# Nine more projections as seven block products, with a ring of three weight slots

## The reference

```
# first block
h = norm(x);  proj = h @ w_in            # q_a k_a v_a q_i k_i w_i z_a c_q c_kv k_rope z_b q_m z_m gates(3*1024)
o_a = top-k sparse attention(q_a, k_a, v_a; index from q_i, k_i, w_i)
o_b = causal attention(norm(c_q) @ w_uq, norm(c_kv) @ w_ukv, k_rope)
kv_m = norm(mem) @ w_mem_kv;  o_m = attention(norm(q_m), norm(k_m), v_m)
branch_n = (o_n * silu(z_n)) @ w_branch[n]
merged = sum_n sigmoid(gate_n) * branch_n
x = x + merged @ w_out
# second block
u = norm(x);  dq, dk, dv, gq, gk, gv, gg, gr = split(u @ w_in_2)
z = gr @ gate_w + gate_b;  log_a = log_sigmoid(z) / 16
L = cumsum(log_a in chunks of 64);  Lc = L - L[middle]
a = where(lower, (q e^Lc)(k e^-Lc)^T, (q e^-Lc)(k e^Lc)^T)
og = a @ v + inter-chunk state;  gla = norm(og) * silu(gg)
da = softmax attention(q1,k1,dv) - lam * softmax attention(q2,k2,dv), q and k normed by heads
x = x + concat(norm(da), gla) @ w_o
x = x + cross_attention(norm(x), norm(mem_2), w_cq, w_ckv) @ w_co
x = x + hierarchical_moe(norm(x))        # 32 experts, top 2 in the best of 4 groups, 1024 -> 512 -> 1024
```

## Time and profile before

| | |
|---|---|
| Median of the runs | 1144.57 us (1144.38 to 1144.93) |
| Profiled execution | 1144.48 us |
| Its span | 1142.8 us |
| PE busy | 944.0 us, 83% of the span, 4742 records |
| DVE busy | 341.3 us, 30% |
| ACT busy | 175.3 us, 15% |
| POOL busy | 102.6 us, 9% |
| DMA | 290.33 MB, 254 GB/s over the span |

### The profile page before, as it was taken

How to read it: one execution, slowest core, us unless ns; L and a number is a source line. 1 busy time by engine, 2 the same in 40 slices (tenths; PEclk the granted TensorE clock), 3 DMA queues, 4 the chain that set the end, 5 groups by cost and what they waited for, 6 DMA issues and landing times.

```text
span 1142.8 us, 11530 instructions
## 1 busy us (share of the span) xinstructions
PE 944.0 (83%) x4742; PEld 532.3 (47%) x4742; DVE 341.3 (30%) x879; ACT 175.3 (15%) x380; POOL 102.6 (9%) x121
## 2 busy tenths in 40 slices
PE   7999999899999999999999999665655556474737
PEld 3555485679999465455544554221221213131312
DVE  3217934764232221525644523100010101010101
ACT  2114232441000012212311312000000000000000
POOL 2013110135343010100000000000000000000000
PEclk9999999999999999999999999888777869787879
DMA  9546232224444264432208548999999999999996
GB/s 328 175 157 218 83 142 74 74 74 145 151 148 180 81 220 147 147 125 96 74 1 316 205 191 356 428 428 428 427 428 428 427 428 428 427 427 428 428 421 271
DMA packets 64308, 290.33 MB, mean 254 GB/s; under 512 B 9015, under 2 KB 11902, under 8 KB 52222
## 3 DMA queue, kind: packets, MB, share of 16 engines
q1 hardware_dynamic: 63966, 289.04, 63.9%
q10 hardware_dynamic: 288, 0.52, 0.1%
HBM read 288.51 MB, written 1.05 MB: 253 GB/s over the span
## 4 chain that ended last, share of the span: by engine, by line
PE 63%; DMA 28%; DVE 5%; ACT 2%; issue 1%; SPq 0%; DVEq 0%; ACTq 0%
PE ACC L505 24%; PE ACC L520 8%; PE AUX L1038 6%; PE ACC L648 6%; DMA ring<-in_w_e_up_dram 5%; PE ACC L544 4%; PE AUX L1074 4%; DMA BIG<-in_w_e_up_dram 3%; DMA ring<-in_w_e_down_dram 3%; DMA PJ<-in_w_e_up_dram 3%; DMA PJ<-in_w_e_gate_dram 3%; DMA BIG<-in_w_e_down_dram 3%; DMA SQE<-in_w_e_down_dram 3%; DMA SQE<-in_w_e_gate_dram 3%; DMA ring<-in_w_e_gate_dram 3%; PE ACC L930 2%
## 5 line engine op out<-in xcount | busy, mean ns | idle before, releaser
L505 PE MATMUL ACC<-ring,BIG 128*128 128x512 f32 (+2 forms) x384 | 159.1, 574 | 0.2 <-ACT BIG L1531 0.2
L1038 PE MATMUL AUX<-ring,R 128*32 128x512 f32 x416 | 113.3, 708 | 54.0 <-DMA BIG<-in_w_e_up_dram 21.5
L505 PE MATMUL ACC<-ring,R 128*128 128x512 f32 (+1 forms) x296 | 129.2, 591 | 2.8 <-DVE R L1697 2.1
L505 PEld LDWEIGHTS ACC<-ring,BIG 128*128 128x128 f32 x384 | 72.5, 190 | 81.6 <-issue 73.6
L520 PE MATMUL ACC<-BIG,ring 128*128 128x256 f32 (+1 forms) x464 | 106.9, 384 | 0.0
L520 PEld LDWEIGHTS ACC<-BIG,ring 128*128 128x128 f32 (+1 forms) x464 | 84.8, 187 | 16.1 <-issue 4.1
L505 PEld LDWEIGHTS ACC<-ring,R 128*128 128x128 f32 x296 | 55.8, 192 | 65.5 <-issue 64.2
L1038 PE MATMUL AUX<-R 128*32 128x512 f32 x112 | 61.9, 717 | 25.2 <-DMA ring<-in_w_e_gate_dram 14.4
L1038 PE MATMUL AUX<-BIG,R 128*32 128x512 f32 x192 | 55.6, 745 | 28.1 <-DMA PJ<-in_w_e_up_dram 21.3
L2207 DVE SCALAR_TENSOR_TENSOR R<-R,AUX 128x512 f32<-128x512 f32 x8 | 5.5, 686 | 232.5 <-ACT R L1626 232.5
L1038 PEld LDWEIGHTS AUX<-ring,R 128*32 128x32 f32 x416 | 28.3, 129 | 92.9 <-issue 92.9
(11 more groups left out here) (313 smaller groups left out, 1290.1 us busy)
## 6 DMA issues: line engine op xcount, KB each, us to landing
ring<-in_w_in_dram SPq DMA_DIRECT2D x20, 2048.0 KB, 7.8
ring<-in_w_e_gate_dram SPq DMA_DIRECT2D x14, 2048.0 KB, 27.0
ring<-in_w_e_up_dram SPq DMA_DIRECT2D x12, 2048.0 KB, 29.8
ring<-in_w_e_down_dram SPq DMA_DIRECT2D x10, 2048.0 KB, 30.3
BIG<-in_w_e_up_dram SPq DMA_DIRECT2D x8, 2048.0 KB, 32.4
PJ<-in_w_e_gate_dram SPq DMA_DIRECT2D x6, 2048.0 KB, 27.6
BIG<-in_w_e_down_dram SPq DMA_DIRECT2D x6, 2048.0 KB, 27.5
PJ<-in_w_e_down_dram SPq DMA_DIRECT2D x6, 2048.0 KB, 34.6
```

What stands on the lines that cost most here:

```text
L505: mm = nc.tensor.matmul(bank[:, t * 512:t * 512 + width], lhs[:, i, t * P:(t + 1) * P], w[:, i, a:a + width], start=(i == 0), stop=(i == k ...
L1038: mm = nc.tensor.matmul(bank[r, :], M_xt[:, k, r], w[e][:, k, :], start=(k == 0), stop=(k == KD - 1))
```

## The change

Nine more chunks become block products: qm, wout0, wout1, ckv0, dq, dk, gv, ckv1, gg, fifteen with the six gates.

- **Form on PE.** For the nine, the block of the activation is the stationary operand and a block of weights moves past it, 256 columns in one matmul: 28 matmuls of 128x256. The result has tokens on the partitions. The gates keep 56 matmuls of 128x128 (`turned=True`).
- **Ring.** The fourth slot becomes a work area `WS` for S_a, S_b and T_x, so the chunks go through three slots until gg is done; the chunk wo1 is the first in the fourth slot again. ckv3 stands before wo0 and wo1 in the list. wcq0 then waits for ckv2, wcq1 for ckv3. The sums of the second memory's blocks are in R5.
- **Pool.** Each sum of weights is four instructions on 128x256 (`add_steps`). S_b' is now written over w12. Pool makes the sums of x right after the rotary embeddings of the first attention, then those of qm, gate00, gate01 and gate10; clears of QPAD and the causal mask; the sums of gate11 to ckv0; clears of ZT and KEN; dq, dk; QP, QN, KE; gv, ckv1, gg, with the clear of ATT between gg's third and fourth sum, once ckv1 is done.
- **DVE.** `combine` puts the results together in four parts (2, 2, 3 and 1 instructions on 128x256), also for the nine, where ACT drained them before. `row_sums` makes the sums of merged, mem2 and x1 (four on 128x512 each). The low buffer is freed by the third part, the high one by the fourth. Their places: merged's sums, the drain of mem2, wout0's result and its addition to x, rsqrt of mem2, mem2's sums, wout1; ckv0's first two parts before the drain of x1, the other two behind it; dq's before the scans, dk's behind LC and LE, gv's inside the scaling of dq and dk.
- **ACT.** The scale of mem2 is applied after combining (`scale_mem2`), the squares of dq and dk come after the exponentials, gg's tanh is read from SBUF.

The diff, cut to its core:

```diff
-        T_x = R2[:, :].rearrange("p (i k q) -> p i k q", i=4, k=4)
-        S_a, S_b = (R5[:, 2048 + 1024 * i:3072 + 1024 * i].rearrange(...) for i in range(2))
+        block_chunks = ["qm"] + gate_chunks + ["wout0", "wout1", "ckv0", "dq", "dk", "gv", "ckv1", "gg"]
+        WS = slots[RING - 1]
+        S_a, S_b = (WS[:, 1024 * i:1024 + 1024 * i].rearrange("p (k n) -> p k n", k=4) for i in range(2))
+        T_x, T_mem2 = (t.rearrange("p (i k q) -> p i k q", i=4, k=4) for t in (WS[:, 2048:4096], R5[:, 2048:4096]))
...
+        slot_no = [i % (RING - 1) for i in range(c + 3)] + [RING - 1] + [i % (RING - 1) for i in range(c, c + 3)] + [RING - 1]
...
-                if c >= RING:
-                    wait_full(sp, last_job[chunks[c - RING][0]])
+                if slot_before[c]:
+                    wait_full(sp, last_job[slot_before[c]])
...
+                products = [(w11, x[0][0], 0, 0), (w12, x[1][0], 0, 0), (S_a, T[:, 0], 1, 1), (S_b, T[:, 1], 3, 2),
+                            (w21, T[:, 2], 0, 3), (w22, T[:, 3], 0, 4), (w12, x[1][1], 4, 0)]
...
+                            if turned:
+                                mm = nc.tensor.matmul(bank[:, j * P:(j + 1) * P], left[:, k, j * P:(j + 1) * P], right[:, k, :], ...)
+                            else:
+                                mm = nc.tensor.matmul(bank, right[:, k, :], left[:, k, :], start=(k == 0), stop=(k == 3))
...
-            project("dq", XT3)
-            project("dk", XT3)
-            project("gv", XT3)
-            project("ckv1", R2T)
+            project_blocks("dq", XT3, T_x, x1_sums)
+            project_blocks("dk", XT3, T_x, x1_sums)
+            project_blocks("gv", XT3, T_x, x1_sums)
+            project_blocks("ckv1", R2T, T_mem2, mem2_sums)
...
+            def add_steps(out, a, b, op, counter, value):
+                for k in range(4):
+                    ins = g.tensor_tensor(out[:, k, :], a[:, k, :], b[:, k, :], op)
+                ins.then_inc(counter, 1)
+                pool.wait_ge(counter, value)
+
+            def weight_sums(name):
...
+                if c:
+                    pool.wait_ge(block_products, 3 * c - 1)
+                add_steps(S_a, w21, w22, ALU.add, w_sums, 4 * c + 1)
+                add_steps(w21, w11, w21, ALU.subtract, w_sums, 4 * c + 2)
+                add_steps(S_b, S_a, w11, ALU.subtract, w_sums, 4 * c + 3)
+                if name == "gg":
+                    wait_full(pool, "ckv1")
+                    g.memset(ATT, 0.0).then_inc(pads_cleared, 1)
+                pool.wait_ge(block_products, 3 * c + 1)
+                add_steps(w12, w12, S_b, ALU.subtract, w_sums, 4 * c + 4)
...
+                for part in parts:
+                    if part < 3:
+                        dve.wait_ge(block_products, 3 * c + part + 1)
+                    if part == 0:
+                        link(v.tensor_copy(o21, m1))
+                        v.tensor_tensor(o11, m2, o21, ALU.add)
+                    elif part == 1:
+                        link(v.tensor_tensor(o21, m6, o21, ALU.add))
+                        v.tensor_tensor(o12, m5, o21, ALU.add)
+                    elif part == 2:
+                        link(v.tensor_tensor(o22, m7, o21, ALU.add))
+                        v.tensor_tensor(o21, o22, m4, ALU.subtract)
+                        v.tensor_tensor(o22, m5, o22, ALU.add).then_inc(free_sem((name, "low")), 1)
+                    else:
+                        wait_full(dve, name)
+                        v.tensor_tensor(o12, m3, o12, ALU.add).then_inc(free_sem(name), 1)
+                        wait_drained(dve, name)
...
+            for h in range(2):
+                combine(f"wout{h}", by_rows(TMP))
...
+                v.scalar_tensor_tensor(out=part, in0=TMP, scalar=0.25, in1=part, ...).then_inc(x_added, 1)
+                dve.wait_ge(x_added, h + 1)
+                if h == 0:
+                    dve.wait_ge(rows_squared, 4)
+                    rsqrt(2, SMALL[:, 64:66], SMALL[:, 78:80]).then_inc(mem2_scaled, 1)
+                    row_sums(T_mem2, quarters(R2T), mem2_sums)
```

More of the change, by code:

```diff
@@ L643, in project_blocks @@
                     bank = (low if m < 4 else high)[:, 256 * (m % 4):256 * (m % 4) + 256]
-                    if sums:
-                        pe.wait_ge(w_sums, 4 * c + sums)
-                    for j in range(2):
-                        for k in range(4):
-                            mm = nc.tensor.matmul(bank[:, j * P:(j + 1) * P], left[:, k, j * P:(j + 1) * P], right[:, k, :],
-                                                  start=(k == 0), stop=(k == 3))
-                            if m == 6 and (j, k) == (1, 3):
+                    if w_sum:
+                        pe.wait_ge(w_sums, 4 * c + w_sum)
+                    if x_sum:
+                        pe.wait_ge(sums, base + x_sum)
+                    for j in range(2 if turned else 1):
+                        for k in range(4):
+                            if turned:
+                                mm = nc.tensor.matmul(bank[:, j * P:(j + 1) * P], left[:, k, j * P:(j + 1) * P], right[:, k, :],
+                                                      start=(k == 0), stop=(k == 3))
+                            else:
+                                mm = nc.tensor.matmul(bank, right[:, k, :], left[:, k, :], start=(k == 0), stop=(k == 3))
+                            n += 1
+                            last = k == 3 and (j == 1 or not turned)
+                            if m == 6 and last:
                                 mm.then_inc(high_full, 1)
-                            elif last and (j, k) == (1, 3):
+                            elif m in (1, 3, 5) and last:
                                 mm.then_inc(block_products, 1)
@@ L1335, in _ @@
             g.tensor_tensor(KE, kt(GK, 2), kt(EE, 2), ALU.mult).then_inc(gla_products, 1)
+            for name in ("gv", "ckv1", "gg"):
+                weight_sums(name)
             for t in range(TT):
@@ L1516, in _ @@
             act.wait_ge(mem2_scaled, 1)
-            square_rows(3, X3, ZTv, ["wout0", "wout1"])
+            square_rows(3, X3, ZTv, [(x_added, 2)])
             def drain_mem2(key, T3, c):
@@ L1525, in drain_mem2, with scale_mem2 @@
                 last.then_inc(free_sem(key), 1)
-            drain_mem2("ckv0", R1v, 0)
+            def scale_mem2(key, T3, c):
+                wait_drained(act, key)
+                for t in range(TT):
+                    part = T3[:, t, c:c + 512]
+                    last = a_.activation(part, part, ACT.Copy, scale=SMALL[:, 78 + t:79 + t])
+                link(last)
+            scale_mem2("ckv0", R1v, 0)
             drain("gr", [(GRT[:, :], lambda b: b[0:16, 0:S])])
@@ L1925, in _, with combine, m @@
             attention("A")
+            def combine(name, outs, parts=range(4)):
+                c = block_chunks.index(name)
+                low, high = (ACC[acc_no[name, half] % 2] for half in ("low", "high"))
+                o11, o12, o21, o22 = outs
+                def m(bank, i):
+                    ap = bank[:, 256 * i:256 * i + 256]
+                    return ap.rearrange("p (j q) -> p j q", j=2) if len(o11.shape) == 3 else ap
+                m1, m2, m5, m6 = (m(low, i) for i in range(4))
+                m7, m4, m3 = (m(high, i) for i in range(3))
+                for part in parts:
[15 more added lines that the diff above has]
+                        wait_drained(dve, name)
@@ L2041, in _ @@
             v.tensor_copy(KEN[64:128, 1, :, :], kb_[64:128]).then_inc(free_sem("kend"), 1)
[L2043 to L2046 removed]
+            combine("gg", by_rows(GG))
             for c in range(3):
```

220 lines of the change are left out of this document (104 added, 116 removed).

## The result

The changed kernel takes 1139.26 us, the median of 5 runs (1138.97 to 1139.61), against 1144.57 for the kernel before in the same comparison: ratio 0.995, interval 0.9939 to 0.9961. It is 5.3 us faster; forecast were 7.9 (1136.7, range 1126 to 1145). The profiled execution has a span of 1137.2 us, against 1142.8.

The account below looks back on a forecast made before the run. PE work bounds the kernel until 703 us, then 420 us of DMA transfers, unchanged. Fewer products 14.5, relief 4.0 and a load wait 0.9, minus new waits 11.55, give 7.85 us less: 1136.7 us, range 1126 to 1145.

Parts of the forecast that it names:

- Step 1: Nine chunks on PE: 28 matmuls of 128x256 take 12.13 us instead of 13.74, 1.61 us a chunk, 14.5 in all.
- Step 2: Softmax stretch, 187 to 266 us: moving Pool's sums away removes PE's waits for DVE; 4.0 us taken, bounds 0 and 6.6.
- Step 3: Load of wcq1: it waits for ckv3 instead of wo0's last product, so a PE wait of 0.91 us goes.
- Step 4: New PE waits because Pool must deliver four weight sums per chunk, 95% full; sum 11.55 us, bounds 1.1 and 22.6.
- (a): wout1 to ckv0: DVE's addition, rsqrt and row sums, delayed by Pool's pieces, free wout1's low bank late; 2.8 us taken.
- (b): gr and gate_z after ckv0: row sums and x1's drain precede freeing both banks; 0 to 1.5 us, taken 0.75.
- (c): gv's fourth product waits for Pool's third sum, behind QP, QN, KE that collide with DVE; bounds 1.1 and 9.7, taken 5.4.
- (d): ckv1: low bank waits for gv's combination inside the head normalization, and S_b is late; 0 to 4 us, taken 1.6.
- (e): gg: a clear of ATT between its third and fourth sum waits for ckv1; 0 to 2 us, taken 1.
- A: Rival: sharing costs little, DVE's operations slip between Pool's pieces; relief 4, waits 3, 1128 us; chance 0.20.
- C: Rival: slower, Pool's queue bounds dq to gg and wout0 to ckv0; waits 22, relief 2, 1149 us; chance 0.10.
- B: Rival: everything comes back and nothing is measured; waits 15.5, relief 1, 1144 us; chance 0.12.

Follow-up runs that it names:

- run 3: Changed kernel with PE's idle time before ckv0 and before gv's fourth product filled by matmuls whose result is thrown away; 1137.98 us.
- runs 2 and 3: First: changed kernel with Pool's products QP, QN, KE behind gv's weight sums, 1139.97 us. Second: changed kernel with PE's idle time filled by throwaway matmuls, 1137.98 us.
- run 4: Changed kernel with each of Pool's weight sums as one instruction on 128x1024 in place of four on 128x256; 1148.94 us.
- run 1: Changed kernel with the second memory's reciprocal square root moved behind x1's row sums, out from between wout0's addition and wout1's combination; 1137.06 us.
- run 7: Changed kernel with qm as a plain projection, Pool's sums of x and of gate00 still early; 1140.98 us.

## Why the prediction came out as it did

**Step 1, fewer products: right.** The chain has the new chunks at 12.10 to 12.34 us when PE doesn't wait (forecast 12.13), and qm's row went from 13.95 to 12.30, 1.65 (forecast 1.61). With this rival D, that the products don't get shorter, is out.

**Step 2, Pool's sums leave the attention: right in mechanism, too small.** 4.0 was taken with 6.6 as the upper end; it was 8.3 + 0.2 - 1.65 = 6.9. The working counted the two waits in the earlier trace rows alone, and they gave 3.7. What it left out is 1.4 of other waits (0.7 for ACT, 0.7 for DVE at L1942) and what follows on a wait: the clock at 0.79 in 215 to 223, about 1.7, visible in the stretches of the kernel before had they been cut finely. The earlier trace rows show the stretch with a mean of 0.98, and that was read as the upper level.

**Step 3, the load wait: right**, 0.9 forecast, 0.7 by the table.

**Step 4, the new waits.** The sum of PE's new waits was forecast well, at 11.55, and the trace has 3.48 + 1.45 + 4.94 + 0.42 + 1.64 = 11.9. Place by place: (a) 2.8 forecast, 3.48; (b) 0.75, none; (c) 5.4, 6.4; (d) 1.6, 0.4; (e) 1, 1.6. Two are too high and three too low by about as much, so that the sum fits this closely is partly luck. The term that was missing is the clock after them, 1.7 + 2.4 = 4.1 us. With it and 1.3 in small pieces, which no run takes apart, the table gives 5.3 and 12.0 us returned, 17.3 in all. This adds up one trace and is not what each term would give back: by run 3 the slow clock at gv alone is worth nothing, as DVE would then have made PE wait 3.0 us at ckv1, a wait forecast at 1.6 in (d). The same omission stood on both sides: 2.9 us more were gained than forecast, and 5.7 more returned; the difference, 2.8, is about the miss of 2.6 (7.9 forecast, 5.3 measured). That the two omissions cancel in part is luck, too.

In (a) the count of two short steps to a piece was wrong. It came from Pool instructions of 1.26 us; with quarters of 0.7 nearly every step waits, and the three with one input in SBUF too, which were counted as free. In (c) the collision was put at the three products; it was at the scans before them and at gv's sums behind them. Which engine is late at gv is not one question: runs 2 and 3 show that with Pool's wait or PE's slow clock removed, DVE is 3 to 10 us late at the next buffer. The rule cited in the prediction, of the Trainium skill, "SBUF — State Buffer", "Who interferes with whom", and the traces agree in the full block: an operation of 0.16 us waits 0.4 to 0.5 us beside pieces of 0.7 and up to 2.1 us beside pieces of 2.35 (run 4).

**The rivals.** A (sharing costs nothing much, 3 us of waits) is refuted by 11.9. C (Pool's queue the bound, slower) is closer to the truth than its 0.10: dq to gg alone is slower than before by 3.9 us, and in run 4 the whole is. B had the size of the returned time about right (15.5, was 17.3) and was wrong in the relief (1, was 6.9).

Of the signs that the prediction named for these steps, no wait for DVE between 187 and 240 is over 0.5 us (0.3), there is none for wcq1, and the new waits lie between its 5 and 17 us.

**One to one to the end: right**, but for 0.7 us: 4.9 us at the first waiting expert load, 5.6 in the spans.

Left open: why the clock fell after a wait of 1.70 us in run 1 and not after one of 1.64 in the changed kernel, or of 3.47 in run 7; and how much of the 2.3 us left over in the first part comes from the quarters.

## What to carry to other kernels

When a change removes or adds waits of TensorE, look up the granted clock behind each wait in stretches of a few microseconds: here 12 us of new waits came with 17 us of lost time, and 5 us of removed ones (7.2 before, 2.2 after, from 187 to 266) with 7 gained. Treat the clock as a range and not as a fixed price, since the same wait of 3.5 us cost 1.7 us in one kernel and nothing in the next; and ask what stands behind it, since at gv its loss was hidden behind VectorE. Before GpSimd is given work that runs all the time, list what VectorE must finish meanwhile on the path to the next buffer, and count a wait of up to one GpSimd instruction for each of its operations with two inputs in SBUF, and for TENSOR_SCALAR and the scan; and let those instructions be short. A conversion that saves 1.6 us of TensorE can lose where such a list is longest: leaving one of nine chunks as it was gave more (9.5 us) than all nine had (5.3).
